# Experts' tile loop written out and reordered, last stage rebuilt on plain gathers

## What is computed

```python
act = jax.nn.silu(hg) * hu * combine[:, :, None]            # gate and up products, 16 experts of width 256
ff  = jnp.einsum('nef,efd->nd', act, w_down)                # combine is 0 but for the two chosen experts
x   = layer_norm(ALPHA * x + (1 + g2) * ff, ln2_g, ln2_b)   # mean, variance, gain, offset over 1024
```

## Time and profile before

| what | value |
|---|---|
| timed runs, median of 3 | 1502.25 us (1501.28 to 1505.97) |
| profiled execution | 1498.89 us, its span 1497.2 us |
| busy, share of the span | PE 86%, DVE 84%, ACT 55%, POOL 46% |
| PE in the attention stage | 90% or more in every slice from 194 to 784 us |
| the experts' stage | first turn at 897.8 us, last store landed at 1375.1 us |
| the last stage | 1375.1 us to 1497.2 us |

### The profile page before, as it was taken

How to read it: one execution, slowest core, us unless ns; L and a number is a source line. 1 busy time by engine, 2 the same in 40 slices (tenths; PEclk the granted TensorE clock), 3 DMA queues, 4 the chain that set the end, 5 groups by cost and what they waited for, 6 DMA issues and landing times. The chain is left out here.

```text
span 1497.2 us, 25357 instructions
## 1 busy us (share of the span) xinstructions
PE 1282.3 (86%) x7959; PEld 709.8 (47%) x7959; DVE 1264.3 (84%) x3123; ACT 823.2 (55%) x1446; POOL 681.6 (46%) x514
## 2 busy tenths in 40 slices
PE   5488799999999999999995438999999999995774
PEld 3355455555555555555543234444544444442221
DVE  2526799999999999999996578999999999994698
ACT  2413244445555555554454117998889988884122
POOL 0112246777776676666763421222222222211786
PEclk9888899999999999999997758999999999998798
DMA  9964442111111111111110396569993554222896
GB/s 311 314 217 161 145 133 71 57 43 57 57 58 58 57 57 40 47 43 57 43 38 39 112 315 229 209 227 347 337 363 112 189 190 152 103 109 91 211 270 193
DMA packets 106687, 219.38 MB, mean 147 GB/s; under 512 B 11796, under 2 KB 71000, under 8 KB 104547
## 3 DMA queue, kind: packets, MB, share of 16 engines
q1 hardware_dynamic: 82662, 141.23, 27.8%
q0 software_dynamic: 11808, 43.00, 10.2%
q10 hardware_dynamic: 12125, 34.01, 5.9%
HBM read 166.68 MB, written 51.56 MB: 146 GB/s over the span
## 5 line engine op out<-in xcount | busy, mean ns | idle before, releaser
L1165 DVE SCALAR_TENSOR_TENSOR y_sum<-uT,w_dw_cols,y_sum 128x128 f32<-128x128 f32 (+1 forms) x1780 | 461.1, 341 | 0.0
L2095 DVE SCALAR_TENSOR_TENSOR w_gate_up_lo<-w_gate_up_ring,w_gate_up_hi 128x2048 f16<-128x2048 f16 x96 | 219.4, 2287 | 33.6 <-ACT w_gate_up_hi L2017 33.4
L2017 ACT ACTIVATE w_gate_up_hi<-w_gate_up_ring 128x2048 f16 x96 | 182.7, 1905 | 52.0 <-issue 51.3
L1998 POOL COPY slot_index<-slot_token 128x1 int32 (+1 forms) x48 | 55.9, 1164 | 309.4 <-PE eturn L2159 305.0
L1403 PE MATMUL bank<-w_in_hi,hT_hi 128*128 128x512 f16 (+3 forms) x544 | 194.4, 357 | 0.9 <-DVE hT_lo L1305 0.9
L1403 PE MATMUL bank<-w_in_lo,hT_hi 128*128 128x512 f16 (+3 forms) x544 | 193.9, 357 | 0.0
L1403 PE MATMUL bank<-w_in_hi,hT_lo 128*128 128x512 f16 (+3 forms) x544 | 193.9, 357 | 0.0
L2138 PE MATMUL ps_up<-w_gate_up_hi,slot_rowsT_hi 128*128 128x512 f16 x384 | 147.2, 383 | 25.4 <-DVE slot_rowsT_lo L2120 25.1
L2138 PE MATMUL ps_up<-w_gate_up_lo,slot_rowsT_hi 128*128 128x512 f16 x384 | 146.7, 382 | 0.0
L2138 PE MATMUL ps_up<-w_gate_up_hi,slot_rowsT_lo 128*128 128x512 f16 x384 | 146.6, 382 | 0.0
L2126 DVE SCALAR_TENSOR_TENSOR w_down_lo<-w_down_ring,w_down_hi 128x2048 f16<-128x2048 f16 x48 | 109.6, 2282 | 4.2 <-ACT w_down_hi L2071 3.9
(11 more groups left out here) (298 smaller groups left out, 2856.5 us busy)
## 6 DMA issues: line engine op xcount, KB each, us to landing
expert_rows<-out_rows ACTq DMA_DIRECT2D x48, 512.0 KB, 2.8
late<-in_w_ada SPq DMA_DIRECT2D x22, 1024.0 KB, 7.5
w_gate_up_ring<-in_w_gate SPq DMA_DIRECT2D x16, 1024.0 KB, 8.5
w_gate_up_ring<-in_w_up SPq DMA_DIRECT2D x16, 1024.0 KB, 11.0
w_down_ring<-in_w_down SPq DMA_DIRECT2D x16, 1024.0 KB, 13.1
x_h<-in_x_prompt SPq DMA_DIRECT2D x16, 512.0 KB
x_res<-in_x_prompt SPq DMA_DIRECT2D x16, 512.0 KB, 3.5
hidden<-late SPq DMA_DIRECT2D x16, 512.0 KB, 2.6
```

What stands on the lines that cost most here:

```text
L1165: dve.scalar_tensor_tensor(total, u, w, y_sum[:, c, :n], ALU.mult, ALU.add).then_inc(taps_done, 1)
L1998: pool.tensor_copy(index[:, c:c + 1], K["slot_token"][:, tile_at(j)]).then_inc(index_ready, 1)
L2017: act.activation(gate_up_parts[0][:, at, k:k + KD // 2, :, :].rearrange("p k a n -> p (k a n)"), w_gate_up[:, bass.ds(b, 1), k:k + KD // 2 ...
L2095: dve.scalar_tensor_tensor(flat[1], w_gate_up[:, bass.ds(b, 1), k, :, :].rearrange("p b k a n -> p (b k a n)"), W_SCALE, flat[0], ALU.mult ...
```

## The change

Experts: the loop is gone, all 51 steps are written out on each engine; within a step the turn of the next tile comes ahead of its fellow stages on PE, ACT and DVE. Last stage: two plain gathers for each tile into two places; DVE adds them, then multiplies by the gate; PE lays the residual rows of three tiles ahead of the first gated tile, and always three tiles ahead after that; ACT copies from PSUM with a sum and squares with a sum; DVE adds eps, POOL raises to the power, and DVE makes gain and offset in two full-width operations, two tiles behind. Rings: gathers 6 tiles of two places instead of 7 of one, output rows 5 instead of 3.

```diff
-        def over_tiles(eng, body):
-            over_steps(eng, body, tiles=SLOT_TILES)
+        def over_tiles(body):
+            for i in range(SLOT_TILES + 3):
+                body((0, i))
...
@@ step of ScalarE @@
                     if turn_tile is not None:
                         split(KD // 2)
-                        act.activation(gate_tanh[:], ps_up[c][:, 0, :], ACT.Tanh, ...).then_inc(tanh_ready, 1)
                     if turn_tile is not None:
                         for h in range(2):
                             act.wait_ge(turned, count(2, j, h + 1))
                             act.copy(rowsT[0][:, c, 4 * h:4 * h + 4, :], turn[h][:, :, :]).then_inc(rowsT_hi_ready, 1)
+                        act.wait_ge(up_done, count(1, j, 1))
+                        act.activation(gate_tanh[:], ps_up[c][:, 0, :], ACT.Tanh, ...).then_inc(tanh_ready, 1)
...
@@ step of VectorE @@
                     if turn_tile is not None:
                         split(1)
-                        dve.scalar_tensor_tensor(gate[:], gate_tanh[:], 1.0, ps_up[c][:, 0, :], ALU.add, ALU.mult).then_inc(gate_ready, 1)
-                        dve.scalar_tensor_tensor(act_tok[:], gate[:], 1.0 / (W_SCALE * W_SCALE), ps_up[c][:, 1, :], ALU.mult, ALU.mult).then_inc(act_ready, 1)
                         for h in range(2):
                             dve.tensor_tensor(rowsT[1][:, c, k, :], turn[h][:, :, :], rowsT[0][:, c, k, :], ALU.subtract).then_inc(rowsT_ready, 1)
+                        dve.scalar_tensor_tensor(gate[:], gate_tanh[:], 1.0, ps_up[c][:, 0, :], ALU.add, ALU.mult).then_inc(gate_ready, 1)
+                        dve.scalar_tensor_tensor(act_tok[:], gate[:], 1.0 / (W_SCALE * W_SCALE), ps_up[c][:, 1, :], ALU.mult, ALU.mult).then_inc(act_ready, 1)
...
@@ step of TensorE @@
+                    if turn_tile is not None:
+                        pe.wait_ge(gathered[c], half(j) * 16 + 16)
+                        for h in range(2):
+                            pe.wait_ge(rowsT_ready, count(2, j, h - 1))
+                            for k in range(4):
+                                mm = pe.transpose(turn[h][:, k, :], rows[:, c, 4 * h + k:D:KD], ident[:])
                     if up_tile is not None:
                         product(ps_up[c] ...)
-                    if turn_tile is not None:
-                        pe.wait_ge(gathered[c], half(j) * 16 + 16)
-                        for h in range(2):
-                            pe.wait_ge(rowsT_ready, count(2, j, h - 1))
-                            for k in range(4):
-                                mm = pe.transpose(turn[h][:, k, :], rows[:, c, 4 * h + k:D:KD], ident[:])
...
-PICK_RING, Y_RING, SUM_RING = 7, 3, 4
+PICK_RING, Y_RING, SUM_RING = 6, 5, 4
...
@@ last stage, POOL @@
+                def pick(t):
+                    b = t % PICK_RING
+                    if t >= PICK_RING:
+                        pool.wait_ge(added, 2 * (t - PICK_RING) + 2)
+                    for s in range(2):
+                        pool.indirect_dma_start(out=picked[:, b, s, :], ..., in_=expert_rows[:, :], ...).then_inc(both_picked[b], 16)
+                for t in range(PICK_RING - 1):
+                    pick(t)
+                for t in range(TILES):
+                    if t + PICK_RING - 1 < TILES:
+                        pick(t + PICK_RING - 1)
+                    pool.wait_ge(eps_added, t + 1)
+                    pool.tensor_tensor(small[:n, b, 4:5], small[:n, b, 3:4], mhalf[:n, :], ALU.pow).then_inc(rstd_ready, 1)
@@ last stage, ScalarE @@
+                act.activation(rows[:, 2, :], rows[:, 2, :], ACT.Copy, scale=D ** 0.5).then_inc(gain_scaled, 1)
+                for t in range(TILES):
+                    act.wait_ge(added, 2 * t + 2)
+                    if t >= Y_RING:
+                        act.wait_ge(y_stored[yb], 16 * (t // Y_RING))
+                    if t >= 4:
+                        act.wait_ge(offset_added, t - 3)
+                    act.activation(y[:n, yb, :], ps_v[t % SUM_RING][:n, :], ACT.Copy, accum_out=small[:n, b, 0:1]).then_inc(copied, 1)
+                    act.wait_ge(copied, t + 1)
+                    act.activation(small[:n, b, 1:2], small[:n, b, 0:1], ACT.Copy, scale=-1.0 / D).then_inc(mean_ready, 1)
+                    act.wait_ge(mean_ready, t + 1)
+                    act.activation(square[:n, :], y[:n, yb, :], ACT.Square, bias=small[:n, b, 1:2], accum_out=small[:n, b, 2:3]).then_inc(squared, 1)
@@ last stage, VectorE @@
+                def gate(t):
+                    dve.wait_ge(both_picked[b], 32 * (t // PICK_RING + 1))
+                    dve.tensor_tensor(picked[:n, b, 0, :], picked[:n, b, 0, :], picked[:n, b, 1, :], ALU.add).then_inc(summed, 1)
+                    dve.wait_ge(summed, t + 1)
+                    dve.tensor_tensor(picked[:n, b, 0, :], picked[:n, b, 0, :], rows[...], ALU.mult).then_inc(gated, 1)
+                def variance(t):
+                    dve.wait_ge(squared, t + 1)
+                    dve.tensor_scalar(small[:n, b, 3:4], small[:n, b, 2:3], D * EPS_SCALED, None, ALU.add).then_inc(eps_added, 1)
+                def norm(t):
+                    dve.scalar_tensor_tensor(y[:n, yb, :], y[:n, yb, :], small[:n, b, 1:2], rows[:n, 2, :], ALU.add, ALU.mult).then_inc(gained, 1)
+                    dve.wait_ge(rstd_ready, t + 1)
+                    dve.wait_ge(gained, t + 1)
+                    dve.scalar_tensor_tensor(y[:n, yb, :], y[:n, yb, :], small[:n, b, 4:5], rows[:n, 3, :], ALU.mult, ALU.add).then_inc(offset_added, 1)
+                for t in range(TILES + 2):
+                    if t >= 2:
+                        variance(t - 2)
+                    if t < TILES:
+                        gate(t)
+                    if t >= 2:
+                        norm(t - 2)
@@ last stage, TensorE @@
+                for t in range(SUM_RING - 1):
+                    residual(t)
+                for t in range(TILES):
+                    pe.wait_ge(gated, t + 1)
+                    for h in range(2):
+                        pe.matmul(v[:n, cols], ident[:n, :n], picked[:n, b, 0, cols], start=False, stop=True).then_inc(added, 1)
+                    if t + SUM_RING - 1 < TILES:
+                        residual(t + SUM_RING - 1)
```

## The result

The changed kernel takes 1483.30 us (median of four runs, 1482.87 to 1483.51) against 1502.21 (1501.28 to 1505.97): a ratio of 0.9874, with an interval of 0.9860 to 0.9888. The forecast was 1479, in a range of 1466 to 1495. Its direction, its mechanism and its split between the two stages held; it was 4.3 us too fast. The profiled execution took 1483.51, its span 1481.8 us.

What follows compares the result with a forecast made beforehand. The experts were taken as bound by a two-step circle of hand-overs (gain 0), the last stage by VectorE (23.0 us less): 1502.25 - 23.0 = 1479 us, range 1466 to 1495.

Steps and rivals of the forecast that it cites:

- The circle: Experts' loop: two-step hand-overs over ScalarE, VectorE and TensorE, 12.87 + 6.45 = 19.32 us against 19.30 before; gain 0.
- What is late next: Experts' step: VectorE's own sum with nothing waited for, 9.41 us, the floor if the hand-overs are shorter.
- S to T: Experts: start of ScalarE's second weight split of a tile to that tile's tanh; forecast 12.87 us, before 11.78.
- Code loading: Experts' written-out steps: loading their code priced at 0; without cover, 1 us stalls each step, up to 45 us.
- Last stage, head: Start of last stage: residual products at half clock, second gather landing after 4.32 us; VectorE's third step waits until 1392.4.
- the case of full clock: Start of last stage: with TensorE at full clock throughout, VectorE's third step would begin at 1389.6, not 1392.4.
- Last stage, 15 steps: Last stage: VectorE bounds each tile at 4.85 us, and 15 such steps reach 1465.2.
- Tail: End of last stage, after 1465.2: tile 16's square, small add, gain, power, offset, then 3.7 us store; end 1474.2.
- The power beside VectorE: Last stage: POOL's power, 0.94 us, costs VectorE's two-operand operations nothing, against the Trainium skill's rule.
- rival D: Last stage: POOL's reads hold VectorE for 0.94 us in each of 15 steps; 14 of 23 us go, 1493; chance 0.06.
- E: Last stage bound by the gathers' DMA, 5.3 us a tile; about 10 us won, 1492 to 1502; chance 0.12.
- F: Last stage: TensorE's clock stays at the lower level, 6.84 us a tile; slower, 1506 us; chance 0.08.

Runs made afterwards that it cites:

- gate_first: Changed kernel with VectorE's gate and act_tok put back ahead of the two row remainders; 1466.43 us, ratio 0.9759 against the kernel before.
- load_ahead: Changed kernel with ScalarE's register load for the down split moved ahead of the casts; 1471.65 us, ratio 0.9784 against the kernel before.
- both edits: Changed kernel with the edits of gate_first and load_ahead together; 1457.99 us, ratio 0.9704 against the kernel before.
- fewer_weights: Changed kernel loading only the first half of the gate and up rows for experts 4 to 15, output wrong; single run 1477.37 us.
- written_old_order: Changed kernel with the experts written out but in the old order; 1476.18 us, ratio 0.9830 against the kernel before.
- last_stage_only: Kernel before with only the new last stage and its rings, experts as before; 1479.34 us, ratio 0.9855.
- loop_new_order: Changed kernel with the experts' loop put back around the new order; 1492.99 us, ratio 0.9933 against the kernel before.

## Why the prediction was right, point by point

- **The circle** was forecast as 12.87 + 6.45 = 19.32, and is 13.0 + 6.31 = 19.31. Both halves moved as said (by 1.2 up and by 1.2 down), TensorE's wait went to ps_act, and the experts' stage stayed where it was but for the stall. gate_first and load_ahead show that it is a circle, and not a chance agreement. Of the two 0.14 misses, the forward one has the small transposes in it, 0.35 (1140.87 to 1141.22) where I put 0.22; the backward one is ScalarE's issue behind a tanh, 0.33 in place of 0.37, the split behind the store, 0.23 in place of 0.27, and the eviction, 0.22 behind the small activation ahead of it where it had been 0.30 (1141.87 to 1142.09, and 1117.06 to 1117.36 before).
- **What is late next** was forecast as VectorE at 9.41, with both exposed register loads in it. load_ahead, with VectorE's order untouched, comes to 9.43, and its circle gives 9.44. Its steps alternate between 9.35 and 9.50. The 9.35 is VectorE's own sum, in steps in which it waits for nothing but its load (down remainders at 1137.32 and 1146.67), so the forecast 9.41 was 0.06 too long. The mean is the circle's: behind 1149 us all remainders of the second half but one start 2.05 or 2.06 behind their split, and S to T is 13.00. With both edits the step is 9.09: in VectorE's old order the row remainders hide its load again, so the floor was that of one order and not of the work.
- **Weights**: the stall near tile 19 was no term of my sum. It exists in the kernel before as well (435.6 us where the circle gives 434.3), and is 3.2 us in the changed kernel's trace. But the three other traces with the same experts' code have 1.2 to 1.5 us over the circle's 434.5, so it is not shown that the change made it grow. fewer_weights shows that the weights cause it. The 2 us that the medians lack beside the last stage's 20.9 thus have no settled place; the first turn alone lies anywhere from 897.8 to 901.0 us in the twelve traces, with the same code ahead of it.
- **Code loading** at 0: written_old_order, as long as the changed kernel, gains over its loop, so no cost is seen. In the profiles the two queues for instructions moved 1.53 MB in the changed kernel and 1.15 MB in the one before.
- **Last stage, head**: 15.5 us (1380.6 to 1396.10), forecast 17.3. Two errors, of opposite sign. The second gather landed 5.97 us behind its issue, not 4.32; why was not tried. And TensorE's clock, which I let stay low through the head, rose early. Windows of the changed kernel and of the kernel before it:

```profile
1380.50:1387.30 6.80, 6.26 (x7) 1.91 (x8) 0.00 (x0) 1.06 (x1) 4.45 (x5) 0.50 0.54 161
1387.30:1394.00 6.70, 4.84 (x12) 1.63 (x11) 4.88 (x4) 0.55 (x1) 5.17 (x6) 1.00 0.96 364
```

```profile
1375.50:1399.00 23.50, 12.51 (x14) 3.50 (x15) 5.07 (x10) 1.44 (x2) 13.82 (x12) 0.50 0.76 200
```

  TensorE, busy 6.26 of the first 6.8 us with the residual products laid ahead, stood at the lower level (1.2 GHz, granted 0.50) for these 6.8 us only, where it had stood there for 23.5, busy 12.51 of them. I had 1389.6 less the old start, 14.5, as the case of full clock; with 1.65 for the gather it is 16.2, and 15.5 was seen.
- **Last stage, 15 steps** of 5.04 instead of 4.85: 2.85 us more. This is the term that was mis-sized most: the price of the scalar form, for want of a row, was taken as that of the plain one, and the second wait as free.
- **Tail**: 10.1 us from the last full step to the end (1471.7 to 1481.8), forecast 9.0. From the end of that step to the square of tile 16 it is 3.9 and not 2.4. One cause is TensorE's last product, from its timeline:

```profile
1469.24 3.65 PE L2326 MATMUL ps_v<-expert_pick,ident 128*128 128x512 f32 x4 [3.06 <-DVE expert_pick L2285]
```

  It took 3.65 where the one before took 1.99: the granted clock is 0.55 from 1469.2 to 1473.0 us, after 1.00 up to 1469. VectorE's last small add waits 0.83 for the square behind it. From this small add to the offset's end it is 3.1 (forecast 2.9), with POOL's power at 1.52 and not 0.94 on the path, and the last store takes 3.1 and not 3.7.
- In sum: -1.8 + 2.85 + 1.1 = +2.1, and 20.9 us were won where 23.0 were forecast. With the 2 us outside the last stage, that is the 4.3 between 1479 and 1483.3.
- **The power beside VectorE**: VectorE's plain operations take 1.22 with it beside them, as they do without, and it is POOL that is stretched (1.47 where it had 0.94). The Trainium skill, "SBUF — State Buffer", section "Who interferes with whom", says that such a pair contends. The trace agrees that there is a contention (1.47 against 0.94), and in this kernel it lies on the other side from the one on which rival D had it.
- **The ground on which D got 0.06** was a misreading, so the low chance was not earned, though D did not come. The gating pair at 1401.35 takes 1.28, but this is not what it takes elsewhere in the kernel before. Its timelines of DVE and POOL:

```profile
1406.21 2.85 DVE L2317 TENSOR_TENSOR expert_pick<-expert_pick,final_rows 128x512 f32<-128x512 f32 x2
1406.60 1.30 POOL L2275 TENSOR_TENSOR y_rows<-y_rows,final_rows 64x512 f32<-64x512 f32 x1
```

  Ten of the 17 gating pairs take 1.54 to 2.85, and they are the ten that run beside POOL's half of the offset by more than 0.1 us; the other seven take 1.27 to 1.29. What the ten take beyond 1.28 is 8.5 us in sum. There it is VectorE that is stretched. The change takes this half from POOL, and no term of the forecast had that; what part of it lay on the path isn't shown.
- **E and F**: the DMA share is 0.83 and not 1, so E was not seen. The granted clock is 1.00 from 1400 to 1469, so F was not seen as a state of the stage; it fell only for the last product (above).

## What to carry to other kernels

Where several engines are busy for nine tenths of a step and none is full, look for the shortest loop of hand-overs, over two steps if the pipeline has two buffers, and add it up from starts in the timeline: an edit is worth what it takes out of that loop divided by the number of steps that it spans, as long as no engine's own sum is longer, and moving work from one half of it to the other is worth nothing. Cost the issue work (register loads, second semaphore waits) as part of it, and take it out of the place behind a wait, where nothing hides it. When an engine's next operation has another form than the rows you price it from, give the term a range of a few per cent for each repetition.

## What the hardware showed that I had not expected

- **A POOL instruction that starts inside a VectorE operation on two SBUF operands ends a fixed time behind it.** The timeline of POOL in the last stage of the changed kernel:

```profile
1416.49 1.47 POOL L2254 TENSOR_TENSOR f_small<-f_small,mhalf 128x1 f32<-128x1 f32 x1 [0.64 <-DVE f_small L2290]
1418.15 1.51 POOL L2244 DMA_INDIRECT expert_pick<-expert_rows,pair_slot  x1 [0.19 <-issue]
```

  The power takes 1.47 where it took 0.94, beside VectorE's add of two SBUF operands at full width. In the experts' stage it is plainer: the issue of the row gather has the same form in both kernels, and its group of lines between 1000 and 1300 us reads (busy us, then mean ns) in last_stage_only, then in the changed kernel:

```profile
L2001 POOL DMA_INDIRECT slot_rows<-hidden,slot_index x31 | 29.8, 962 | 24.7 <-POOL slot_index L1998 24.7
```

```profile
L1990 POOL DMA_INDIRECT slot_rows<-hidden,slot_index x31 | 69.7, 2248 | 24.4 <-POOL slot_index L1987 24.4
```

  The issue falls beside VectorE's row remainder from PSUM in the old order, and beside the weight remainder of two SBUF operands in the new one: 0.96 against 2.25 us. loop_new_order, which has the new order in a loop, shows 2.20 too, so it is the neighbour and not the code. The starts and ends of the changed kernel say more. All 44 issues of the row gather from 918 us on start inside a weight remainder, and all end 0.83 to 0.85 us behind that remainder's end, whether they started 0.11, 0.58 or 0.91 into it (3.02, 2.54 and 2.21 us long). The 17 powers end 0.40 to 0.43 behind the end of the operation in which they started. The gather issue at 1419.96 starts 0.14 ahead of the offset and takes 0.94 beside it. So it is the operation in progress at the start that counts, and not one that starts later. It costs nothing in the experts' stage, where POOL idles. VectorE's own operations keep their durations in both stages of this kernel (2.28 to 2.29, 1.21 to 1.23 and 1.27 to 1.29), unlike in the kernel before, where POOL's work beside them was longer. What in the chip is the reason was not tried.
- **A register load behind a waiting instruction** costs 0.33 us on ScalarE and 0.34 on VectorE, as idle time that the profile calls issue. Moved ahead of work that is queued, it costs nothing visible. On ScalarE that took 0.22 us off a step and 9.0 us off tiles 2 to 47 (437.7 to 428.7).
- **The granted clock** at the head of the last stage turned from 0.50 to 1.00 after 6.8 us, of which TensorE was busy 6.26, and in the kernel before after 23.5 us, of which it was busy 12.51. In the changed kernel it fell back to 0.55 at 1469.2 us, after two stretches of 5 us with TensorE busy 1.98 and 1.99 us in each, and a product took 3.65 us instead of 1.99.
